# Feature-major tokens and vectors laid out on the host, the first weights loaded in halves, and the first two blocks multiplied in halves

## The reference

```python
meta = jnp.broadcast_to(meta_tokens.astype(x.dtype)[None], (b, N_META, D_MODEL))
h = jnp.concatenate([meta, x], axis=1)
...
hn = rms_norm(h, g_mix[layer])
h = h + attention_mixer(hn, cos, sin, w_in_attn[j], g_cq[j], w_uq[j], g_ckv[j], ...)
...
def attention_mixer(h, cos, sin, w_in, ...):
    z = h @ w_in
    c_q, c_kv, k_pe, fq, fk, fv, f_logit = jnp.split(z, _offsets(ATTN_SPLITS), axis=-1)
```

## Time and profile before

| What | us |
|---|---|
| Median of three runs | 1226.09 (1225.68 to 1226.25) |
| Profiled execution, its own time | 1228.11 |
| Span of the profiled execution | 1226.3 |
| TensorE busy with matmuls | 1207.4 (98%) |
| VectorE busy | 903.5 (74%) |
| ScalarE busy | 714.1 (58%) |
| GpSimd busy | 249.4 (20%) |

### The profile page before, as it was taken

The page is one execution under the profiler, slowest core; times in us unless marked ns, Lnnn a source line. Parts: engine busy times, 40 slices in busy tenths (PEclk is TensorE's granted clock), DMA queues, the critical chain, the costliest instruction groups (busy, mean ns, idle before and its releaser), DMA issues.

```text
span 1226.3 us, 23640 instructions
## 1 busy us (share of the span) xinstructions
PE 1207.4 (98%) x8096; PEld 1103.9 (90%) x8096; DVE 903.5 (74%) x1562; ACT 714.1 (58%) x1303; POOL 249.4 (20%) x260
## 2 busy tenths in 40 slices
PE   7999999999999999999999999999999999999997
PEld 5998899999999988888889998888889998888886
DVE  5788886555557988776569869776667988878764
ACT  4657756664444556664447877665445797666343
POOL 3100014220000114440011003442002811444000
PEclk9999999999999999999999999999999999999999
DMA  7514326655557555655556426655555644665550
GB/s 225 161 36 132 106 81 199 201 172 178 196 176 224 187 187 180 199 175 186 190 179 200 160 81 210 200 176 196 179 172 172 207 138 143 218 186 190 181 197 35
DMA packets 194922, 208.79 MB, mean 170 GB/s; under 512 B 6159, under 2 KB 183565, under 8 KB 194717
## 3 DMA queue, kind: packets, MB, share of 16 engines
q1 hardware_dynamic: 191861, 202.73, 51.6%
q10 hardware_dynamic: 2984, 5.06, 1.3%
HBM read 206.69 MB, written 2.64 MB: 171 GB/s over the span
## 4 chain that ended last, share of the span: by engine, by line
PE 86%; DVE 7%; ACT 3%; issue 2%; DMA 1%; DVEq 0%; ACTq 0%; SPq 0%
PE PS L1934 27%; PE PS L1935 14%; PE PS L1928 10%; PE PS L1929 10%; PE PS L1930 10%; PE PS L2511 2%; PE PS L2512 2%; PE PS L2513 2%; DVE wlo L1081 2%; PE PS L2113 1%; PE PS L2179 1%; PE PS L2157 1%; ACT whi L535 1%; PE PS L2275 1%; PE PS L2273 1%
## 5 line engine op out<-in xcount | busy, mean ns | idle before, releaser
L1081 DVE TENSOR_TENSOR wlo<-raw,whi 128x1024 fp32r<-128x1024 f32 x370 | 455.3, 1237 | 159.1 <-ACT whi L535 156.2
L535 ACT ACTIVATE whi<-raw 128x1024 fp32r<-128x1024 f32 x370 | 388.7, 1053 | 313.0 <-PE PS L1935 170.2
L1934 PE MATMUL PS<-x,whi 128*128 128x512 f32 x832 | 291.5, 395 | 0.5 <-DVE x L1058 0.5
L1935 PE MATMUL PS<-x,wlo 128*128 128x256 f32 x832 | 234.4, 282 | 0.0
L1928 PE MATMUL PS<-x,whi 128*128 128x258 f32 (+2 forms) x800 | 232.7, 291 | 1.1 <-DVE wlo L1081 0.8
L1929 PE MATMUL PS<-x,whi 128*128 128x258 f32 (+2 forms) x800 | 228.6, 286 | 0.0
L1930 PE MATMUL PS<-x,wlo 128*128 128x258 f32 (+2 forms) x800 | 228.1, 285 | 0.0
L1934 PEld LDWEIGHTS PS<-x,whi 128*128 128x128 f32 x832 | 156.3, 188 | 36.4 <-DVE x L1058 0.8
L1837 POOL TENSOR_TENSOR act_s<-act_r 128x256 f32<-128x256 f32 (+1 forms) x128 | 143.3, 1120 | 212.3 <-ACT act_r L597 150.3
L1934 PE MATMUL PS<-hid,whi 128*128 128x512 f32 x512 | 179.8, 397 | 0.2
L1817 POOL TENSOR_TENSOR acc<-acc,sq 128x256 f32<-128x256 f32 (+2 forms) x64 | 52.6, 823 | 589.9 <-ACT sq L579 252.5
(11 more groups left out here) (323 smaller groups left out, 2010.8 us busy)
## 6 DMA issues: line engine op xcount, KB each, us to landing
raw<-in_mlp_w SPq DMA_DIRECT2D x64, 1024.0 KB, 5.3
raw<-in_w_mlp_up SPq DMA_DIRECT2D x32, 1024.0 KB, 5.5
raw<-in_w_mlp_down SPq DMA_DIRECT2D x32, 1024.0 KB, 5.0
raw<-in_w_in_conv SPq DMA_DIRECT2D x12, 1024.0 KB, 5.1
raw<-in_attn_w_in SPq DMA_DIRECT2D x12, 1024.0 KB, 5.1
raw<-in_mlstm_w_in SPq DMA_DIRECT2D x12, 1024.0 KB, 5.7
raw<-in_w_in_attn SPq DMA_DIRECT2D x9, 1024.0 KB, 5.5
raw<-in_w_out_attn SPq DMA_DIRECT2D x4, 1024.0 KB, 5.1
```

The lines of the kernel that those rows point to most:

```text
L535: A(part_view(whi, b), raw_view(b), ACT.Copy).then_inc(w_hi, 1)
L1081: V.tensor_tensor(part_view(wlo, b), raw_view(b), f32(part_view(whi, b)), ALU.subtract).then_inc(w_lo, 1)
L1934: mm(dst.rearrange("p (a t) -> p a t", a=2), std_cols(whi[b % RING], k), xs_both, start=first, stop=False)
L1935: return mm(dst[:, S:2 * S], std_cols(wlo[b % RING], k), xs_hi, start=False, stop=last)
```

## The change

The host part, `kernel()`, puts the meta tokens and x together and lays them out as [128, 8, 272], features on the partitions (`h_in`); it makes one array of the identity and the two vector tables, turned (`vecs`), and one of the relative bias and its one-hot table (`rel_in`). The kernel loads these in place, so that the transposes, their copies and three of the loads go. `h_in` comes in two DMAs by halves of the slices k, and so does raw0. TensorE runs 24 matmuls on ones (`WARM`) while it would wait. The splits of blocks 0 and 1 are made in halves, and TensorE runs the left half (k 0 to 3) of blocks 0 and 1, then the right half of both. ACT makes the squares after all the rounded parts of the tokens; blocks 4 and 5 get banks 6 and 7, so no block up to 5 waits for a read; all splits up to block 7 are made ahead of the norm, whose matmul moves from behind block 1 to behind block 3. `rel_rows` lies in `act_r`, and its readers wait for `rel_mm`, `rel_read` and `rel_out`.

```diff
+            if o in (4, 5):
+                return o + 2
             return (o + 1) % PSR if o < A_LEAD or o >= O["a_om"] else (o + 1) % 2
...
-            sp.dma_start(x_tok[:, :, :], d["x"][0].rearrange("(a p) n -> p a n", p=P)).then_inc(Z["x_in"], 16)
-            sp.dma_start(meta_tok[:, :], d["meta_tokens"]).then_inc(Z["x_in"], 16)
-            sp.dma_start(vrow_a[:, :], d["v_rows_a"]).then_inc(Z["vec_in"], 16)
-            sp.dma_start(vrow_b[:, :], d["v_rows_b"]).then_inc(Z["vec_in"], 16)
+            for n in range(2):
+                ks = slice(n * KB // 2, (n + 1) * KB // 2)
+                sp.dma_start(h_parts[:, ks, :], d["h_in"][:, ks, :]).then_inc(Z[("x_in", "x_right")[n]], 16)
...
-            linear("a_in", wa, [fq, fk])
+            for n in range(2):
+                ks = slice(n * KB // 2, (n + 1) * KB // 2)
+                sp.dma_start(std(raw[0][:, :])[:, ks, :], kpn(wa)[:, ks, fq:fq + 2 * P]).then_inc(raw_ready[0] if n else Z["w_half"], 16)
+            load(G["a_in"] + 1, kpn(wa)[:, :, fk:fk + 2 * P])
...
+            act.dma_start(vecs[:, :], d["vecs"]).then_inc(Z["const_in"], 16)
+            act.dma_start(rel_in[:, :], d["rel_in"]).then_inc(Z["rel_in"], 16)
...
+            def x_high(k):
+
+                act.wait_ge(Z["x_in" if k < KB // 2 else "x_right"], 16)
+                A(at(xh, k, FULL), at(h, k, FULL), ACT.Copy, scale=gain(0, k)).then_inc(Z["x_hi"], 1)
+
+            def x_square(k):
+
+                act.wait_ge(Z["acc_ready"], max(k, 1))
+                A(sq[:, k % 2, 0:T], at(h, k, FULL), ACT.Square).then_inc(Z["sq_ready"], 1)
+
+            def first_hi(b, half):
+
+                act.wait_ge(raw_ready[0] if half else Z["w_half"], 16)
+                A(half_view(part_view(whi, b), half), half_view(raw_view(b), half), ACT.Copy).then_inc(w_hi if half else Z["w_first"], 1)
+
+            act.wait_ge(Z["const_in"], 16)
+            for half in range(2):
+                for k in range(half * KB // 2, (half + 1) * KB // 2):
+                    x_high(k)
+                for b in range(2):
+                    first_hi(b, half)
             for k in range(KB):
-                residual(0, k, FULL, (Z["pro_ev"], N_PRO + k + 1))
-                if k == 2:
-                    split_hi(0)
-            for b in range(1, RING):
+                x_square(k)
+                if k in (1, 4):
+                    split_hi(2 + k // 4)
+            for b in range(4, 8):
                 split_hi(b)
...
-                split_hi(B["a_in"] + j + RING)
+                if j >= 4:
+                    split_hi(B["a_in"] + j + RING)
...
+            V.tensor_copy(wlo[RING - 1][:, 0:2 * P].rearrange("p (a c) -> p a c", a=2), ones[:, :].unsqueeze(1).broadcast_to((P, 2, P)))\
+                .then_inc(Z["const_set"], 1)
...
+            for half in range(2):
+                for k in range(half * KB // 2, (half + 1) * KB // 2):
+                    low_part(0, k, FULL)
+                for b in range(2):
+                    first_lo(b, half)
+            split_lo(2)
+            dve.wait_ge(Z["rel_mm"], 1)
+            V.tensor_scalar(rel_rows, PS[0:HEADS, 5, 0:3 * P], float(DV) ** 0.5, None, ALU.mult).then_inc(Z["rel_read"], 1)
+            split_lo(3)
...
+            for b in range(4, 8):
+                split_lo(b)
             norm(0, FULL)
...
-                if j < A_LEAD - 1:
+                if 4 <= j < A_LEAD - 1:
                     split_lo(B["a_in"] + j + RING)
...
+            pe.wait_ge(Z["const_set"], 4)
+            for _ in range(WARM):
+                mm(PS[:, 7, 0:2 * P], wlo[RING - 1][:, 0:P], wlo[RING - 1][:, 0:2 * P], start=True, stop=True)
             pe.wait_ge(Z["const_in"], 16)
...
+            pe.wait_ge(Z["rel_in"], 16)
+            mm(PS[0:HEADS, 5, 0:3 * P], rel, onehot, start=True, stop=True).then_inc(Z["rel_mm"], 1)
...
-            for j in range(A_LEAD):
+            for some in (range(KB // 2), range(KB // 2, KB)):
+                for j in range(2):
+                    pe.wait_ge(w_lo if some[0] else Z["w_first_lo"], j + 1)
+                    for k in some:
+                        if j == 0:
+                            pe.wait_ge(Z["x_ready"], k + 1)
+                        last = product(B["a_in"] + j, k, std_cols, at(xh, k, FULL), at(xl, k, FULL), PS[:, a_bank(j), 0:T],
+                                       k == 0, k == KB - 1)
+                    if some[-1] == KB - 1:
+                        last.then_inc(w_used, 1)
+            for j in range(2, A_LEAD):
...
-                if j == 1:
+                if j == 3:
                     norm(0, T)
```

More of the change, by code:

```diff
@@ L188, in build @@
         h = sb("h", [P, KB * T])
+        h_parts = h[:, :].rearrange("p (k t) -> p k t", k=KB)
         x2, y2 = sb("x2", [P, KB * 2 * T], F32R), sb("y2", [P, KB * 2 * T], F32R)
         xh, xl, yh, yl = (x2, 0), (x2, T), (y2, 0), (y2, T)
-        ident, ones = sb("ident", [P, P]), sb("ones", [P, P])
-        vrow_a, vrow_b = sb("vrow_a", [na, P]), sb("vrow_b", [nb, P])
-        vec_a, vec_b = sb("vec_a", [P, na]), sb("vec_b", [P, nb])
+        ones, vecs = sb("ones", [P, P]), sb("vecs", [P, P + na + nb])
+        ident, vec_a, vec_b = vecs[:, 0:P], vecs[:, P:P + na], vecs[:, P + na:P + na + nb]
         eps = sb("eps", [P, 2])
@@ L211, in build @@
         with ExitStack() as s:
-            x_tok, meta_tok = sb("x_tok", [P, TS, D], F32, s), sb("meta_tok", [N_META, D], F32, s)
-            onehot, rel = sb("onehot", [BUCKETS + 1, 3 * P], F32, s), sb("rel", [BUCKETS + 1, HEADS], F32, s)
-            rel_rows = sb("rel_rows", [HEADS, 3 * P], F32, s)
+            rel_in = sb("rel_in", [BUCKETS + 1, HEADS + 3 * P], F32, s)
+            rel, onehot = rel_in[:, 0:HEADS], rel_in[:, HEADS:HEADS + 3 * P]
             lam_in, lam_tmp = sb("lam_in", [P, 4, DV], F32, s), sb("lam_tmp", [P, 2, DV], F32, s)
@@ L653, in _ @@
             A(lam[:, 2:4], lam[:, 0:2], ACT.Exp).then_inc(Z["lam_exp"], 1)
-            act.dma_start(rel_dram, rel_rows[:, :]).then_inc(Z["rel_out"], 16)
-            act.wait_ge(Z["pro_t"], N_PRO + KB)
+            act.wait_ge(Z["rel_read"], 1)
+            act.dma_start(rel_dram, rel_rows).then_inc(Z["rel_out"], 16)
+            act.wait_ge(Z["rel_mm"], 1)
             act.dma_start(amask[:, :], d["c_mask"]).then_inc(Z["mask_in"], 16)
@@ L2037, in mlp @@
                         last.then_inc(w_used, 1)
+            pe.wait_ge(Z["const_set"], 4)
+            for _ in range(WARM):
+                mm(PS[:, 7, 0:2 * P], wlo[RING - 1][:, 0:P], wlo[RING - 1][:, 0:2 * P], start=True, stop=True)
             pe.wait_ge(Z["const_in"], 16)
-            pe.wait_ge(Z["const_set"], 4)
-            pe.wait_ge(Z["vec_in"], 32)
-            nc.tensor.transpose(PS[:, 0, 0:na], vrow_a[:, :], ident[0:na, 0:na]).then_inc(Z["pro_t"], 1)
-            nc.tensor.transpose(PS[:, 1, 0:nb], vrow_b[:, :], ident[0:nb, 0:nb]).then_inc(Z["pro_t"], 1)
-            pe.wait_ge(Z["rel_in"], 32)
-            mm(PS[0:HEADS, 2, 0:3 * P], rel[:, :], onehot[:, :], start=True, stop=True).then_inc(Z["pro_t"], 1)
-            pe.wait_ge(Z["x_in"], 32)
-            for k in range(KB):
-                cols = slice(k * P, (k + 1) * P)
-                if k >= 4:
-                    pe.wait_ge(Z["pro_ev"], N_PRO + k - 3)
-                nc.tensor.transpose(PS[:, 4 + k % 4, 0:N_META], meta_tok[:, cols], ident[0:N_META, 0:N_META])
-                for a in range(TS):
-                    last = nc.tensor.transpose(PS[:, 4 + k % 4, N_META + a * P:N_META + (a + 1) * P], x_tok[:, a, cols], ident[:, :])
-                last.then_inc(Z["pro_t"], 1)
+            pe.wait_ge(Z["rel_in"], 16)
+            mm(PS[0:HEADS, 5, 0:3 * P], rel, onehot, start=True, stop=True).then_inc(Z["rel_mm"], 1)
             def a_free(o):
                 back = PSR if o < A_LEAD or o >= O["a_om"] + 4 else 2
+                if o < 6:
+                    return
                 if 2 <= o - O["a_om"] < 4:
@@ L2553, in rows @@
         return _np.concatenate(table)
-    data = {"v_rows_a": rows(VEC_A), "v_rows_b": rows(VEC_B), **shape_constants()}
-    for name in ("x", "meta_tokens", "w_in_attn", "w_uq", "w_ukv", "w_out_attn", "w_in_conv", "w_out_conv", "w_mlp_up",
-                 "w_mlp_down", "rel_bias_2", "attn_w_in_2", "attn_lambda_q1_2", "attn_lambda_k1_2", "attn_lambda_q2_2",
+    consts = shape_constants()
+    data = {"v_rows_b": rows(VEC_B), **{name: consts[name] for name in ("c_cos", "c_sin", "c_mask")}}
+    tokens = _np.concatenate([_np.asarray(inputs["meta_tokens"]), _np.asarray(inputs["x"])[0]])
+    data["h_in"] = tokens.reshape(T, KB, P).transpose(2, 1, 0)
+    data["vecs"] = _np.concatenate([consts["c_ident"], rows(VEC_A).T, rows(VEC_B).T], axis=1)
+    never = _np.full((1, HEADS), NEG, _np.float32)
+    data["rel_in"] = _np.concatenate([_np.concatenate([_np.asarray(inputs["rel_bias_2"]), never]), consts["c_onehot"]], axis=1)
```

(2 more changed lines are left out.)

41 lines of the change are left out of this document (12 added, 29 removed).

## The result

| | us | ratio to before (95%) |
|---|---|---|
| before, median of 20 | 1226.43 (1225.68 to 1227.62) | |
| after, median of 20 | 1228.52 (1227.60 to 1229.93) | 1.0017 (1.0011 to 1.0023) |

The account below looks back on a forecast made before the run. TensorE, holding 86% of the chain that ended last, bounds the kernel. Block 3's end at 24.1 plus 13.1 starts block 7 at 37.2 instead of 41.76, gaining 4.6 us: 1221.5 us, chance 0.46, range 1218.3 to 1223.9.

Parts of the forecast that it names:

- Removed: At the start: transposes, their eight DVE copies and the path from 7.8 to 16.1 go, with three loads.
- ring: Rival: SP held at the load for blocks 7 and 8, block 7's split waits 8.4 us; 1229.9 us, chance 0.06.
- First half, 9.3, first product 10.6: Start: raw0's left half lands at 9.3 us; after half splits and handovers the first product starts at 10.6, against 16.1.
- The 0.9 us for the hole in the DMA engines' work: Early loads: removing three loads was counted to bring the weights 0.9 us earlier, bounds 0 and 1.5.
- stated lower bound of 7.7: Earliest landing allowed for raw0's left half: 7.7 us, half of raw1's 3.3 behind x.
- low clock: Rival: after idling, TensorE runs 18 matmuls at the low level, costing 1.8 us; gain 4.1, 1222.0 us, chance 0.24.
- Blocks 2 and 3, E = 24.1: Raw1 lands at 15.7, block 2 starts at 18.1, and block 3 ends at 24.1 us, called E.
- wait of 1.3: Ahead of block 2: TensorE idle 1.3 us, waiting for raw1 and its split.
- The chain of 13.1 behind E: From block 3's end through split, lam, rstd and refinement to the second head_sums: 13.1 us, TensorE itself needing 10.4.
- From lam to Ln 1.70: Behind block 3 on ACT: lam exponent, rel_dram store and three mask loads ahead of rstd's Ln, 1.70 us.
- 2.7: Ahead of the second head_sums: TensorE waits, giving back 2.7 us of the lead; bounds 0 and 4.8.
- 4.6 predicted at block 7: Block 7 starts at 37.2 us instead of 41.76, a gain of 4.6 us.

Follow-up runs that it names:

- after_hid32: Changed kernel with 32 unused bytes in front of hid2 alone, putting hid2, h_tok and o_gain back on multiples of 64 bytes; ratio to before 0.9972.
- before_hid32: Kernel before with 32 unused bytes in front of hid2 alone, putting hid2, h_tok and o_gain 32 bytes off; 1228.52 us against 1226.71.
- pad32_lam: after_pad32 with the four small lam_in loads issued behind the first splits of blocks 0 and 1 instead of ahead; 1221.51 us.
- after_again: The changed kernel measured once more, nothing altered; 1227.85 us against 1227.10 for the kernel before, ratio 1.0008.
- pad32_warm56: after_pad32 with 56 warming matmuls in place of 24; 1223.32 us.
- pad32_early: after_pad32 with the sums of squares behind block 2, the norm ahead of the splits of blocks 6 and 7, and ACT's token work first; 1222.44 us.
- before_again: The kernel before measured once more for a second trace, nothing altered; ratio 1.0001.
- after_pad32: Changed kernel with an unused 32-byte tile per partition behind eps, putting later tiles back on multiples of 64 bytes; 1223.79 us against 1227.33 before.
- after_pad1056: Changed kernel with an unused 1056-byte tile per partition behind eps, putting every later tile back where it was before; 1223.58 us against 1227.33 before.
- before_pad32: Kernel before with an unused 32-byte tile behind eps, putting later tiles 32 bytes off a multiple of 64; ratio 1.0005.
- after_cold: Changed kernel without its 24 warming matmuls; ratio to before 1.0002.

## Why the prediction was wrong

The sign failed on a term that the prediction put at nothing without a reason: what removing tiles costs elsewhere. The steps it has gave about half their sum.

- *What the removal costs elsewhere.* "Removed" counts the transposes, copies and loads, and nothing for the tiles that go with them. Removing five tiles moved all later ones, and `hid2` onto 32 bytes off a multiple of 64: +2.48 us, shown by after_hid32 and before_hid32. The placement costs another 1.67 from 550 to 590 and from 840 to 888, which any pad took away; its mechanism is open. Together this is 4.15. None of the rivals had it; "ring", the only slower one, didn't happen.
- *First half, 9.3, first product 10.6.* Landed at 10.6, first product 11.99. The 0.9 us for the hole in the DMA engines' work was laid to the loads that go. The hole came from `lam_in`'s small rows, which stay: pad32_lam has the landing at 8.2 (1.66 + 6.5). The stated lower bound of 7.7 lies 0.5 under that.
- *The clock.* The rival "low clock" came true: the level was high until 10.7, fell during the idle time, and 24 matmuls ran low (18 were predicted, at 1.8 us; they cost 2.4). In after_again only 14 did, behind a first product at 12.95, and block 3 ended at 26.64, as late as in after. Its own argument, that the wait for raw1 takes most of it, held as well: pad32_warm56 wins only 0.1 at block 7, less than the traces scatter. Part 1 of "TensorE: Matmul & The Clock Gate" in the Trainium skill names the low level as the idle default, and the 0.85 and 0.50 of the granted clock behind the idle time agree.
- *Blocks 2 and 3, E = 24.1.* E was 26.59, 2.5 later: 1.4 by the first product and 2.4 by the clock, less the wait of 1.3. That wait ahead of block 2 did not show, because the low clock brought TensorE to it at 20.56. With a high clock it is there, 1.49.
- *The chain of 13.1 behind E.* Right in kind and place: the releaser and the line are those forecast. By the same marks it took 12.7 (12.4 to the first product, which the prediction put 0.36 later). Two terms were off. From lam to Ln 1.70 were counted and 0.68 were measured from the split's end, since DMA issues overlap with the running activation; the split came at E + 1.33 and not 1.09. The refinement was at E + 3.0, not 3.9. Other steps took 0.4 longer. The wait was 1.9 instead of 2.7, and pad32_early, which takes it away, brings block 7 forward by 1.4.
- *Sum.* 4.6 predicted at block 7, 2.4 measured: E 2.5 later, the chain 0.3 shorter. Behind it, by after's trace: +1.67 and +2.48 by the placement and +0.30 in the parts not shown, which with the -2.42 makes +2.03. What moves in steps is left out of this. The pair after_again and before_again, in which the steps fell nearly alike, gives 2.04; the medians say 2.1 in one comparison and 0.75 in the other. So of the 6.7 us between forecast and result, 2.1 lie in the start and 4.15 in the placement.
- *The range*, 1218.3 to 1223.9, was made of the start alone. after_pad32 with 1223.79 lies in it: with the placement kept the change is worth 3.5 us against its before of 1227.33, where 4.6 were forecast and 4.1 for "low clock".

## What to carry to other kernels

When a change drops or adds a tile, work out where every later tile lands, and keep the operands that TensorE loads as weights on the same offset from a multiple of 64 bytes as before; the pads in after_pad32 and after_pad1056 cost no time that shows. It is no guarantee: 32 bytes off a multiple of 64 doesn't explain the 1.67 us, so look at every stage again. If a trace shows TensorE busy all the time at the full clock, compare the number of matmuls in equal windows, since a slower pace has no idle time to be seen in. At a kernel's start, look at the small transfers on other queues before the large ones, and let a warm-up reach to the first product or leave it out.

## What the runs showed of the hardware

- A stationary operand (f32, 128 columns) that starts 32 bytes off a multiple of 64 made 512-column matmuls follow each other at 0.2333 us instead of 0.2267 (2.48 over 384), with no wait and a granted clock of 1.00. The same offset of a moving operand alone showed no cost in before_hid32.
- Two stretches of matmuls with `hid2` as the moving operand ran 0.77 and 0.90 us longer in the three traces of the changed kernel's own placement, and 0.00 in the 16 others, before_pad32 with the same offsets from 64 bytes among them. The cause was not found.
- Four broadcast loads of 32 KB in rows of 256 bytes on ACT's queue held a 1 MB load on SP's queue back by 3.9 us (14.0 from issue in after_pad32, 10.1 in pad32_lam).
- In after, behind 6.4 us of matmuls and 4.1 of idle time, the granted clock was 0.50 at the first product and 1.00 again 5.5 us later (3.5 in after_again); after_cold, without the 5.5 us of warm-up, began at the same spacing of 0.226.
- Four DMA issues on ACT's queue beside a running activation cost 0.3 us together, not their 1.6.
- Executions of one kernel differ by steps of about 0.8 us: 0.79 and 0.84 from 41 to 273, 0.75 in the stage at 840; what sets them was not found.
